# A transformer forward pass in fp32: mixed attention by pairs of heads between parts of query units, penalty on TensorE

## What is computed

```python
(qa, ka, va, qb, kb, vb, qc, ckv, qidx, kidx, widx) = _split_cols(h @ w_in[l])
out_a = _sliding_window_attn(qa, ka, va, attn_sinks[l], tab_a)   # 8 heads, window 128, 2 key/value heads
out_b = _moba_attn(qb, kb, vb, tab_b)                            # 4 heads; with T=512 all past keys are kept
kv_c = _rmsnorm(ckv, kv_norm_c[l]) @ w_kv_up_c[l]
out_c = _dsa_attn(qc, kv_c[..., :64], kv_c[..., 64:], qidx, kidx, widx, tab_c)
#   4 heads; score = sum_h relu(qidx . kidx) * widx; the 128 best keys of each query are kept
x = x + jnp.concatenate([out_a, out_b, out_c], axis=-1) @ w_out[l]
```

## Time and profile before

| | us |
|---|---|
| median of 3 runs (3419.64 to 3426.7) | 3426.13 |
| the profiled execution | 3420.45 |
| its span | 3418.2 |
| TensorE busy in the span | 3279.7 (96%) |
| VectorE busy | 1843.0 (54%) |
| ScalarE, GpSimd busy | 1168.2, 492.6 |
| mean granted clock of TensorE | 0.973 |

### The profile page before, as it was taken

The page is one execution under the profiler, slowest core; times in us unless marked ns, Lnnn a source line. Parts: engine busy times, 40 slices in busy tenths (PEclk is TensorE's granted clock), DMA queues, the critical chain, the costliest instruction groups (busy, mean ns, idle before and its releaser), DMA issues.

```text
span 3418.2 us, 42576 instructions
## 1 busy us (share of the span) xinstructions
PE 3279.7 (96%) x14746; PEld 2619.5 (77%) x14746; DVE 1843.0 (54%) x2784; ACT 1168.2 (34%) x1935; POOL 492.6 (14%) x466
## 2 busy tenths in 40 slices
PE   7999998999999999998999989879999999999998
PEld 5888776688888888775888868657888886678887
DVE  3434486543445444685543443577747555577474
ACT  4322225332223222334322221454424325444242
POOL 0000323400020001133200030013000323220003
PEclk8999998999999999989999999999999999999998
DMA  3434430133333333320333333102333231123332
GB/s 107 132 112 130 122 86 13 49 99 98 92 101 90 104 92 102 80 62 1 95 107 87 101 100 88 49 13 68 100 96 95 84 88 44 41 71 99 92 102 76
DMA packets 541423, 287.83 MB, mean 84 GB/s; under 512 B 14419, under 2 KB 537398, under 8 KB 541328
## 3 DMA queue, kind: packets, MB, share of 16 engines
q1 hardware_dynamic: 535936, 273.32, 27.7%
q0 software_dynamic: 5392, 13.31, 1.4%
HBM read 284.30 MB, written 10.02 MB: 86 GB/s over the span
## 4 chain that ended last, share of the span: by engine, by line
PE 82%; DVE 8%; ACT 4%; issue 3%; POOL 1%; DMA 1%; DVEq 0%; ACTq 0%; POOLq 0%
PE bank L1755 68%; PE bank L1801 2%; PE bank L1866 1%; PE bank L1932 1%; PE bank L1990 1%; PE bank L1964 1%; DVE norm_t L1250 1%; DVE w_lo L1177 1%; PE bank L1769 1%; ACT probs L873 1%; PE bank L1785 1%; PE bank L2002 1%; ACT w_hi L674 1%; DVE proj L1558 1%; DVE probs L1457 1%
## 5 line engine op out<-in xcount | busy, mean ns | idle before, releaser
L1755 PE MATMUL bank<-h_hi,w_hi 128*128 128x512 f32 x2864 | 1123.9, 392 | 14.3 <-DVE w_lo L1177 12.6
L1755 PE MATMUL bank<-h_lo,w_hi 128*128 128x512 f32 x2864 | 1116.8, 390 | 0.0
L1755 PE MATMUL bank<-h_hi,w_lo 128*128 128x512 f32 x2864 | 1116.4, 390 | 0.0
L674 ACT ACTIVATE w_hi<-w_raw 128x1024 fp32r<-128x1024 f32 (+2 forms) x477 | 533.6, 1120 | 1550.0 <-PE bank L1755 899.0
L1177 DVE TENSOR_TENSOR w_lo<-w_raw,w_hi 128x1024 fp32r<-128x1024 f32 (+2 forms) x461 | 641.0, 1392 | 489.9 <-ACT w_hi L674 489.7
L1755 PEld LDWEIGHTS bank<-h_hi,w_hi 128*128 128x128 f32 x2864 | 538.1, 188 | 139.8 <-issue 20.5
L1755 PEld LDWEIGHTS bank<-h_lo,w_hi 128*128 128x128 f32 x2864 | 538.3, 188 | 114.0 <-issue 2.1
L1755 PEld LDWEIGHTS bank<-h_hi,w_lo 128*128 128x128 f32 x2864 | 538.2, 188 | 113.0
L1755 PE MATMUL bank<-act_hi,w_hi 128*128 128x512 f32 x924 | 359.4, 389 | 0.0
L1755 PE MATMUL bank<-act_lo,w_hi 128*128 128x512 f32 x924 | 359.4, 389 | 0.0
L1755 PE MATMUL bank<-act_hi,w_lo 128*128 128x512 f32 x924 | 359.4, 389 | 0.0
(11 more groups left out here) (301 smaller groups left out, 3482.8 us busy)
## 6 DMA issues: line engine op xcount, KB each, us to landing
w_raw<-in_ffn_w_gate_dram SPq DMA_DIRECT2D x88, 512.0 KB, 3.8
w_raw<-in_ffn_w_up_dram SPq DMA_DIRECT2D x88, 512.0 KB, 3.8
w_raw<-in_ffn_w_down_dram SPq DMA_DIRECT2D x64, 704.0 KB, 4.7
w_raw<-in_ffn_w_in_dram SPq DMA_DIRECT2D x88, 512.0 KB, 3.8
w_raw<-in_ffn_w_out_dram SPq DMA_DIRECT2D x32, 704.0 KB, 4.7
w_raw<-in_w_in_dram SPq DMA_DIRECT2D x34, 512.0 KB, 3.7
w_raw<-in_a_w_qkv_dram SPq DMA_DIRECT2D x24, 512.0 KB, 3.8
w_raw<-in_w_out_dram SPq DMA_DIRECT2D x16, 512.0 KB, 4.0
```

Source lines behind the costliest of these rows:

```text
L674: nc.scalar.activation(w_hi[c % 2][:, 0:nk, 0:cols], raw[c % 2][:, 0:nk, 0:cols], ACT.Copy).then_inc(hi_ready, 1)
L1755: mm = nc.tensor.matmul(result(c)[0:cols, :], w[b][:, k, 0:cols], x[:, k, :], start=(k == 0 and n == 0), stop=(k == nk - 1 and n == 2))
```

## The change

- **Mix in slots.** The fox slots become general by a plan per pair (`pair_plan`). Four local pairs are narrow: two phases of two tiles, two turn groups. Projection units are reordered (`W_IN_ORDER`): keys and values first, the 8 query units last. Units 11 to 17 run inside slots -1 to 5, as do parts of output units 0 and 1 in slots 6 and 7 (`LAST_FILL`). Pair p's output goes to `O_HI`, `O_LO` in buffers of their own.
- **Penalty.** The selection writes 0 or -2^103 into `pen` in single-pass form; TensorE adds it to the scores of the sparse pairs with an identity. GpSimd's adds go.
- **Rounds.** 18 of the 48 rounds run beside units 5 to 10, 30 in slots -1 to 4.
- **Scaling** is issued by phase as its exponentials are done: tiles 2 and 3 on VectorE, 0 and 1 on GpSimd. GpSimd makes the low parts of units 4 to 19. ScalarE alone copies the turned probabilities of local and block heads.
- **Fox**: the same slots with the last two filled, no stash, values turned beside units 11 to 17.
- **Start**: units 0 and 1 one after the other, unit 0's weight parts made among the copies of x, the statistic ahead of the low parts, `channel_rows` after the first down unit, tables into banks of their own, a bias row per unit.
- The ffn input after mix no longer waits block by block for the output units.

```diff
+WIDE = dict(phases=[[(3, 0)], [(2, 0), (0, 3 * P)], [(1, 0)]], ...
+            groups=[(0,), (1, 3), (2,)], ... parts=[[0, 1], [2, 3], [4, 5]])
+NARROW = dict(phases=[[(3, 0), (2, NEAR)], [(1, 0), (0, NEAR)], []], ...
+            groups=[(0, 2), (1, 3)], ... parts=[[0, 1], [2, 3], []])
...
+    plan["act_groups"] = range(len(plan["groups"])) if early else (0, 2)
+    plan["pool_tiles"] = (0, 1)
...
-        POOL_LOW = range(10, 18)
-        PACE = 2
+        POOL_LOW = range(4, MIX_Q + NP + 2)
+        ROUNDS = {5: 2, 6: 3, 7: 3, 8: 8, 9: 13, 10: 18}
+        SLOT_ROUNDS = [22, 26, 30, 34, 40, 48]
...
-            def select(h):
...
+                    for p in range(NP):
+                        if MIX_Q + p + 2 in POOL_LOW:
+                            low(BASE[name] + MIX_Q + p + 2)
+                        pair_scale(name, p)
...
-                        nc.vector.tensor_scalar(tile, tile, TAKEN / 2, MASKED / SCALE, ALU.is_gt,
+                        nc.vector.tensor_scalar(pen[:, off(t):off(t + 1)], tile, TAKEN / 2, LEFT_OUT, ALU.is_gt,
                                                 ALU.mult).then_inc(pen_ready, 1)
...
+            def pair_slots(stage, q0, rounds):
                 for p in range(-1, NP):
                     nxt = p + 1 < NP
+                    if p >= 1:
                         pair_low(stage, p - 1)
                     if nxt:
                         pair_max(stage, p + 1, 0)
                     if p >= 0:
                         pair_turned(stage, p, 0)
+                    if p + 3 <= NP + 1 and stage not in MIX:
                         lo(q0 + p + 3)
                     if nxt:
                         pair_max(stage, p + 1, 1)
+                        pair_sums(stage, p + 1, 0)
                     if p >= 0:
                         pair_turned(stage, p, 1)
+                    rounds(p, 0)
+                    if nxt:
+                        pair_max(stage, p + 1, 2)
+                        pair_sums(stage, p + 1, 1)
+                    if p >= 0:
+                        pair_turned(stage, p, 2)
+                    rounds(p, 1)
+                    if nxt:
+                        pair_sums(stage, p + 1, 2)
                     if p + 2 < NP:
+                        at = QP + p + 2 if stage in MIX else 2 * KT + (p + 2) % Q_RING
+                        divided(q0 + p + 2, proj[:, at, :])
                 pair_low(stage, NP - 1)
...
+            FILL = [range(0, 3), range(3, 6), range(6, KT)]
+            LAST_FILL = {NP - 2: [(0, range(0, 3)), (0, range(3, 5)), (0, range(5, 6))],
+                         NP - 1: [(1, range(0, 3)), (1, range(3, 5)), (0, range(6, 7))]}
...
             def pair_slots(stage, q0, count):
                 for p in range(-1, NP):
+                    for part in range(3):
+                        if p + 1 < NP:
+                            if part == 0:
+                                wait_evacuated(pe, q0 + p + 1)
+                            pair_scores(stage, p + 1, part)
+                        if p >= 0:
+                            pair_turn(stage, p, part)
+                        if p + 2 < NP:
+                            gemm_blocks(q0 + p + 2, FILL[part], H_HI, H_LO, h_ready, count)
+                        else:
+                            s, blocks = LAST_FILL[p][part]
+                            gemm_blocks(q0 + NP + s, blocks, *of_heads)
...
                     if p >= 0:
                         pair_values(stage, p)
+                gemm_blocks(q0 + NP + 1, range(5, 7), *of_heads)
+                gemm_blocks(q0 + NP, range(7, KT), *of_heads)
+                gemm_blocks(q0 + NP + 1, range(7, KT), *of_heads)
...
+                            mm = nc.tensor.matmul(PAIR_S[x][:, at:at + w], ident_r[:, :], pen[:, off(i):off(i + 1)],
+                                                  start=False, stop=True)
```

More of the change, by code:

```diff
@@ new lines, in pair_turned @@
+            def pair_turned(stage, p, part):
+                plan = PLAN[stage, p]
+                for s in plan["parts"][part]:
+                    x, n = plan["steps"][s]
+                    if n not in plan["act_groups"]:
+                        continue
+                    at, w = plan["spans"][n]
+                    act.wait_ge(pt_turned, TURNED[stage, p] + s + 1)
+                    act.wait_ge(pv_done, HEAD[stage] + 2 * p)
+                    nc.scalar.activation(PROBS_T2[kind(stage)][x][:, at:at + w], TURN[s % 2][:, 0:w],
+                                         ACT.Copy).then_inc(pt_even, 1)
@@ new lines, in pair_sums @@
+            def pair_sums(stage, p, ph):
+                plan = PLAN[stage, p]
+                if ph not in plan["used"]:
+                    return
+                both = (slice(0, P), pair_rows(stage, p), plan["tiles"][ph])
+                dve.wait_ge(p_ready, NT * (JOB[stage] + 2 * p) + plan["before"][ph + 1])
+                if plan["narrow"]:
+                    dve.wait_ge(sink_ready, HA * MIX[stage] + 2 * p + ph + 1)
+                    chain(nc.vector.tensor_tensor(psum_r[both], psum_r[both], sink_e[both], ALU.add))
+                nc.vector.reciprocal(recip[both], psum_r[both]).then_inc(recip_ready, 1)
+                if ph in plan["dve"]:
+                    dve.wait_ge(recip_ready, INVERTED[stage, p] + plan["used"].index(ph) + 1)
+                    for x in range(2):
+                        n = 2 * p + x
+                        g = JOB[stage] + n
+                        for i, _ in plan["phases"][ph]:
+                            if i not in plan["pool_tiles"]:
+                                tile = ring_of(stage)[n % 4][:, off(i):off(i) + keys(softmax_job(stage, n), i)[1]]
+                                ins = nc.vector.tensor_scalar(tile, tile, recip[:, g % 4, i:i + 1], None, ALU.mult)
+                        ins.then_inc(pl_ready, 1)
@@ L1631, in small_values @@
                 chain(nc.vector.tensor_scalar(nsinks[:, :, :], sinks[:, :, :], -1.0, None, ALU.mult))
+                for i in range(2):
+                    chain(nc.vector.tensor_copy(sinks2[:, :, :, i], sinks[:, :, :]))
                 chain(nc.vector.tensor_scalar(g_sub, g_sub, 1.0 - LAMBDA_INIT, None, ALU.mult))
@@ L2046, in pair_values @@
+                pe.wait_ge(pt_even, BY_ACT[stage, p] + by_act)
+                if by_act < len(plan["steps"]):
+                    pe.wait_ge(pt_odd, BY_DVE[stage, p] + len(plan["steps"]) - by_act)
                 for b in range(NT):
-                    at = SLOT_AT[b]
+                    at = plan["slot_at"][b]
+                    if plan["narrow"] and b:
+                        before = plan["slot_at"][b - 1] + P
+                        for x in range(2):
+                            nc.tensor.matmul(OUT[HD * x:HD * (x + 1), P * b:P * (b + 1)], head_values(stage, 2 * p + x, b - 1),
+                                             turned[x][:, before:before + P], start=True, stop=False)
+                    to = slice(P * b, P * (b + 1) if plan["narrow"] else T)
@@ L2088, in attention @@
[L2088 to L2099 removed]
+                scores(stage, 0)
```

958 lines of the change are left out of this document (436 added, 522 removed).

## The result

The changed kernel takes 3407.01 us (median of five runs, 3404.98 to 3407.34); the kernel before takes 3426.13. The ratio is 0.9946, with a 95% interval of 0.9931 to 0.996. It is faster, by 19 us, where 47 were forecast (3379.5), and it lies above the range, which ended at 3402.

The account below looks back on a forecast made before the run. TensorE, busy 96%, was taken to bound the kernel, with VectorE deciding the new mix slots. Mix -15, start -19 and fox -9.5 made -43.5 against 3420.45, 3377; put towards the median, 3379.5 us, range 3335 to 3402.

Parts of the forecast that it names:

- Mix, -15 forecast: Both mix layers: 7.5 us less a layer, -15 in all, with bounds of -2 and -13 each.
- The clock term: Mix slots: restarts at 1.2 GHz behind TensorE's holes cost between nothing and 10 us a layer; 5 taken.
- The walk: Mix: work and waits summed along VectorE's path through the slots, 152.1 us a layer at full clock against 164.6 before.
- The late weight: Output unit 2, in both mix layers and fox: weights split late, some 2.0 us in mix and 2.3 in fox.
- Start, -19 forecast: Kernel start: first units without the statistic's wait, row work moved later; 19 us less, bounds -14 and -22.
- Fox, -9.5 forecast: Fox: values turned beside units, earlier slot 0, tail of 28.1 for 35.6 us; 9.5 less, bounds -5 and -13.
- Low parts on GpSimd: Units 4 to 19: GpSimd makes low weight parts at 2.40 us each, hidden within a unit's 5.45, costed at nothing.
- the rounds' price: Selection rounds on VectorE: 0.98, 1.25 and 1.51 us at 256, 384 and 512 elements, unchanged beside GpSimd's work.
- the third rival: Mix slots: GpSimd's low parts and scalings slow VectorE's work beside them by 1.54, +65 us a layer, 3510; chance 0.03.
- the second: Mix: holes keep the clock down in most of each slot, second-part scores come late, no gain, 3394.5 us; chance 0.22.
- The fourth rival: Mix and fox: slots serialise on ScalarE's order, fox's tail gains nothing, only the start remains, 3405 us; chance 0.08.
- The first rival: Mix: TensorE sets the slots as VectorE overlaps better, 42 us less a layer, 3296, half of it 3338; chance 0.12.

Follow-up runs that it names:

- Experiment 1: The changed kernel plus matmuls of a finished weight block into an unused bank where TensorE stands still before mix slots 0 to 5: 3391.97 us.
- experiment 4: The changed kernel with mix-slot rounds dealt over three places, 16 instead of 18 ahead of slot -1, second-phase scaling behind the turned-probabilities copy: 3343.68 us, ratio 0.9757.
- experiment 7: The changed kernel without the penalty's matmuls, so the four sparse heads attend to all past keys: 3400.25 us.
- experiment 8: The changed kernel with output unit 0's last block taken before the last values, in both mix layers and fox (result differs): 3393.85 us.
- experiment 2: The changed kernel with VectorE's query unit division and last sums ahead of the second part of each mix slot's rounds: 3377.68 us, ratio 0.9857.
- experiment 3: The changed kernel without the 30 rounds in and just ahead of the mix slots, selection ending after 18 of 48: 3308.47 us.

## Why the prediction was wrong

The sum was -43.5 against the profiled execution; it came out at -14.8. By its own steps:

- **Mix, -15 forecast, +7.6 measured.** This is the step that failed, in two terms of about equal size, the clock and the walk. The clock term was "I take 5, as part falls on fill". Experiment 1 shows 10.3 a layer, the whole upper bound. It falls on fill only in part of a slot: first scores, turns and nine matmuls of the unit stand ahead of the second maxima. The scores and turns ran at 1.2 GHz, and in slot 1 so did four of the nine matmuls (2.88 us for the nine, 2.08 at full clock). I had the row for it, a hole of 2.42 us with 7 us at 0.52 behind it, and six larger holes in my own walk.
- **The walk.** The sum of 152.1 without clock loss holds 2.0 for value turns and the latent projection, and 1.7 of that is spent ahead of the end of unit 10. From the end of unit 10 to the third output unit it says 150.1; taking the 10.3 from the measured 622.67 - 457.4 = 165.3 leaves 155. The 5 us are slot -1 (19.9 for 18.5), slots 0 to 4 (91.0 at full clock for 89.2) and the tail (44.0 for 42.4, of which 0.6 are the late weight's hole and 0.8 the penalty). Of the single slots, the local ones were 0.8 to 1.1 too short and the next two a little too long: 20.3 forecast for slot 3 against 19.8 at full clock, 23.7 for slot 4 against 23.3.
- **The late weight** was priced 2.0; it is a hole of 2.6 and 1.6 to 1.8 of slow clock, in both mix layers and in fox. So in mix_0 a gain of 7.5 became a loss of 2.4: 5.3 for the clock in the slots, 4.9 for the walk, 1.7 for the clock behind the late weight, less 1.6 that the first unit of mix_0 took less than in the kernel before (5.73 us for 7.33). That last part is luck: the change leaves the unit's work as it was, and in five of the eight experiments it takes 7.1 to 8.6.
- **mix_1** lost 2.8 more than mix_0. It lacks that luck, as its first unit takes 5.71 us in both kernels, which is 1.6. And in the kernel before its attention was 1.5 shorter: from the last projection unit (1500.72) to the output units (1613.78) it took 113.1, where the first layer took 114.6.
- **Start, -19 forecast, -18.1 measured.** Right, part by part: units 0 and 1 from 17.77, the statistic at 30.52 (31.7 forecast for its end, 31.38 measured), no hole behind it, the loop at 42.3 (42.6), the rows 3.9 us of TensorE (4.0) and hidden elsewhere.
- **Fox, -9.5 forecast, -9.4 up to the third output unit**, then 1.8 lost to the clock. It was right in sum, not in all its parts: the values' wait for a copy cost 0.35 a slot, which I had not seen (the moved scaling stands ahead of the copy on VectorE's queue).
- **Low parts on GpSimd, the rounds' price.** As costed (and the penalty within 0.4 a pair). In mix_0 of the kernel after, four of the 16 MAX8 of 256 elements lie wholly beside a low part on GpSimd and take 0.43 us, as the other 12 do, so the third rival is out for the rounds. For 384 elements the kernel before has the comparison, and it is smaller than my "beside all of them": six of 16 lie beside a low part, at 0.55 to 0.56 like the rest.

```profile
L1437 DVE MAX8 top<-score 128x8 f32<-128x256 f32 x16 | 6.8, 425 | 0.4
```

Of the rivals, the second (holes keep the clock down, mix gains nothing, 3394.5, chance 0.22) was the one that came true, down to its sign in the trace: local slots over 17 us. Even it was 12.5 too low, as mix did not stay even but lost 7.6 us, and 3.6 us went in unchanged stages and 1.8 behind fox. The fourth rival has the nearest number (3405, chance 0.08) by luck: it lets fox's tail gain nothing and the slots wait for ScalarE, while fox gained 9.4 and the slots wait for VectorE's division. The bounds of the forecast were also added up wrong: the low ends of the four parts are 2, 2, 14 and 5, so the weak end is -23 and not -29. The range to 3402 covers that too. The first rival was excluded for the right reason: the division stood last in each slot. That this was one line's place, to be mended for 14 us a layer, I had not drawn from it.

## What to carry to other kernels

When a walk along one engine shows that another will stand still before each step, charge the slow clock behind every such hole in full, on everything up to the next point where the first engine waits; half was not a safe middle here. In a loop where two engines hand work to each other, put the instruction that the other waits for ahead of filler work, and deal the filler into the waits: here the same work in another order made 3407 us into 3344 (experiment 4). And look at what stands ahead of a hand-over on each queue, even where it is short.

## What the runs showed that I had not expected

- **Unchanged stages differ between kernels.** The differential attention does the same in all ten kernels. From the end of its last value copy to its output units it takes 109.1 us in the kernel before, 111.3 in the one after, 109.2 in experiments 7 and 8, 112.4 in experiments 2, 3 and 4. The first unit of mix_0 stands behind a hole of nearly the same length in the three kernels read for it (2.74 us in the kernel before, 2.87 in the one after, 2.91 in experiment 4), and takes 7.3, 5.7 and 8.6 us. Its first matmul takes 0.50 us in the kernel after and 0.80 in experiment 4, so the slow clock stood behind one of these two holes and not behind the other. Single mix slots differ in the same way: slot 1 takes 17.2 us in the kernel after and 15.8 in experiment 8, whose edit comes later. Where the clock falls and rises changes with what ran earlier; that explanation is read from the lengths and was not tested. The clock, or what else shifts here, makes a single comparison of whole times uncertain by some 3 us, so terms under that are better read from marks.
- **A scaling on VectorE waits for GpSimd.** Two tiles of 512 columns take 0.88 us. In experiment 2, with a low part running on GpSimd from 527.03 to 529.43, they took 2.27, ending 0.69 after it. The mix stages of eight kernels have 21 such meetings in which a pair takes 1.30 to 2.27 us, and each ends 0.67 to 0.69 after the low part. No run was made to test it. Beside GpSimd's own scalings, pairs of 384 columns keep their 0.86. MAX8 beside a low part kept its 0.43, 0.55 and 0.69 for 256, 384 and 512 elements.

```profile
527.85 2.27 DVE L1525 TENSOR_SCALAR probs<-probs,recip 128x512 f32<-128x512 f32 x2
```

```profile
527.03 2.40 POOL L659 TENSOR_TENSOR w_lo<-w_raw,w_hi 128x1024 fp32r<-128x1024 f32 x1 [4.45 <-ACT w_hi L734]
```

The Trainium skill (GPSIMD Engine Reference, Specifications) names contention for VectorE instructions with two SBUF inputs or in a two-port mode. The trace agrees for the scaling, if it runs in such a mode, and for the rounds, which were not slowed. I had used the rule for the rounds alone and not for the scalings, whose price I took from places without a neighbour.
